# Another order for the middle of a hybrid mixer: spectrum, inverse, second transform and query products

## What is computed

```python
for l in range(2):
    x = x + 0.5 * swiglu_ffn(rms_norm(x, ffn1_norm), w_gate, w_up, w_down)
    proj = rms_norm(x, mix_norm) @ w_in
    y_hy = hyena_mixer(proj[hy_in], ...)
    y_mla = mla_mixer(proj[cq], proj[ckv], proj[kr], ...)
    y_gla = gla_mixer(proj[q, k, v, gates, r], ...)
    x = x + concatenate([y_hy, y_mla, y_gla]) @ w_out
    x = x + 0.5 * swiglu_ffn(rms_norm(x, ffn2_norm), ...)
return rms_norm(x, final_norm)

def hyena_mixer(...):                  # two long convolutions, by Fourier transform
    v, x1, x2 = split(short_conv(u))
    z = x1 * fft_long_conv(v, kern[:, 0], skip[0])
    y = x2 * fft_long_conv(z, kern[:, 1], skip[1])
    return rms_norm(y, out_norm)

def mla_mixer(...):                    # 4 heads; q, k = 128 plain + 64 rotated columns
    q = rms_norm(cq) @ w_uq;  q_rope = rope(q[..., 128:])
    k, v = rms_norm(ckv) @ w_ukv;  k_rope = rope(kr)
    return rms_norm(softmax(q @ k.T * scale) @ v, out_norm)

def gla_mixer(...):                    # gated linear attention, forward and backward
    ...                                # decays: running sums of gate logarithms
```

## Time and profile before

| | before |
|---|---|
| median of 3 runs | 1040.7 us (1040.04 to 1040.89) |
| the profiled execution | 1040.12 us, of which 1038.1 us are its span |
| TensorE busy | 1010.4 us (97%) |
| VectorE, ScalarE, GpSimd busy | 637.3, 485.4, 111.6 us |
| granted TensorE clock | full in all 40 slices |
| the middle of layer 1, 258 to 332 us: TensorE busy | 68.92 of 74 us |
| the middle of layer 2, 768 to 842 us: TensorE busy | 68.92 of 74 us |

### The profile page before, as it was taken

The page is one execution under the profiler, slowest core; times in us unless marked ns, Lnnn a source line. Parts: engine busy times, 40 slices in busy tenths (PEclk is TensorE's granted clock), DMA queues, the critical chain, the costliest instruction groups (busy, mean ns, idle before and its releaser), DMA issues.

```text
span 1038.1 us, 17426 instructions
## 1 busy us (share of the span) xinstructions
PE 1010.4 (97%) x7004; PEld 923.8 (89%) x7004; DVE 637.3 (61%) x738; ACT 485.4 (47%) x663; POOL 111.6 (11%) x160
## 2 busy tenths in 40 slices
PE   7999999999899999999999999999998999999997
PEld 6999999888778999999999999997886889999996
DVE  4655555676886655555566555557679765555555
ACT  6544434356654544343354443434566554434342
POOL 2000000150331100000020000003315220000001
PEclk9999999999999999999999999999999999999999
DMA  9565455444303554555555545552542245455551
GB/s 306 188 227 203 167 197 181 143 163 150 135 22 142 202 202 168 197 179 184 183 178 203 203 167 197 179 185 86 199 164 80 81 148 218 167 197 178 186 182 41
DMA packets 27084, 175.93 MB, mean 169 GB/s; under 512 B 3200, under 2 KB 3712, under 8 KB 6560
## 3 DMA queue, kind: packets, MB, share of 16 engines
q1 hardware_dynamic: 25744, 172.90, 46.5%
q0 software_dynamic: 720, 1.95, 0.7%
q10 hardware_dynamic: 576, 0.45, 0.2%
HBM read 174.58 MB, written 1.05 MB: 169 GB/s over the span
## 4 chain that ended last, share of the span: by engine, by line
issue 50%; PE 38%; POOL 9%; DVE 1%; DMA 1%; POOLq 1%; ACT 0%; SPq 0%; DVEq 0%; ACTq 0%
PE psum L1036 13%; PE psum L1037 13%; PE psum L1038 13%; POOL mixer_scratch L350 3%; POOL mixer_scratch L371 1%; POOL mixer_scratch L370 1%; DMA x<-in_x_dram 1%; POOL statistics L323 1%; POOL statistics L321 1%; POOL statistics L334 0%; POOL x_normed L375 0%; DVE x L727 0%; POOL statistics L337 0%; POOLq L226 0%; POOL mixer_scratch L372 0%
## 5 line engine op out<-in xcount | busy, mean ns | idle before, releaser
L681 DVE TENSOR_TENSOR w_low<-w_raw,w_high 128x2048 fp32r<-128x2048 f32 (+1 forms) x160 | 362.8, 2271 | 198.5 <-ACT w_high L409 198.5
L1036 PE MATMUL psum<-xT_high,w_high 128*128 128x256 f32 x1536 | 437.8, 285 | 1.7 <-DVE xT_low L691 1.6
L1037 PE MATMUL psum<-xT_low,w_high 128*128 128x256 f32 x1536 | 435.3, 283 | 0.0
L1038 PE MATMUL psum<-xT_high,w_low 128*128 128x256 f32 x1536 | 435.2, 283 | 0.0
L409 ACT ACTIVATE w_high<-w_raw 128x2048 fp32r<-128x2048 f32 (+1 forms) x160 | 299.1, 1874 | 99.1 <-PE psum L1038 96.3
L1036 PEld LDWEIGHTS psum<-xT_high,w_high 128*128 128x128 f32 x1536 | 295.2, 192 | 5.8 <-issue 4.0
L1037 PEld LDWEIGHTS psum<-xT_low,w_high 128*128 128x128 f32 x1536 | 295.4, 192 | 1.9 <-issue 0.5
L1038 PEld LDWEIGHTS psum<-xT_high,w_low 128*128 128x128 f32 x1536 | 295.4, 192 | 0.0
L457 ACT ACTIVATE silu_gate<-hidden 128x256 f32<-128x256 f32 x88 | 36.8, 418 | 298.9 <-DVE hidden L706 298.9
L1036 PE MATMUL psum<-w_high,hT_high 128*128 128x512 f32 (+1 forms) x360 | 140.0, 389 | 0.0
L1037 PE MATMUL psum<-w_low,hT_high 128*128 128x512 f32 (+1 forms) x360 | 139.7, 388 | 0.0
(11 more groups left out here) (180 smaller groups left out, 801.9 us busy)
## 6 DMA issues: line engine op xcount, KB each, us to landing
w_raw<-in_w_dram SPq DMA_DIRECT2D x160, 1024.0 KB, 4.8
w_raw<-in_w_dram SPq DMA_DIRECT2D x8, 256.0 KB, 7.9
x<-in_x_dram SPq DMA_DIRECT2D x2, 512.0 KB, 5.8
mixer_scratch<-in_fil_dram POOLq DMA_DIRECT2D x2, 512.0 KB, 6.6
out_dram<-x_normed SPq DMA_DIRECT2D x3, 256.0 KB, 2.1
mixer_scratch<-in_fil_dram POOLq DMA_DIRECT2D x2, 352.0 KB, 6.3
mixer_scratch<-in_fin_dram SPq DMA_DIRECT2D x1, 512.0 KB, 5.5
dft<-in_dft_dram SPq DMA_DIRECT2D x1, 256.0 KB, 5.1
```

The source lines that it names most:

```text
L681: e.tensor_tensor(filled(WL[p], n), filled(raw[p], n), filled(WH[p], n).bitcast(F32), ALU.subtract).then_inc(s_lo.sem, 1)
L1036: e.matmul(out, ah, bh, start=start, stop=False)
L1037: e.matmul(out, ah, bl, start=False, stop=False)
L1038: return e.matmul(out, al, bh, start=False, stop=stop)
```

## The change

All functions stay; calls change places, in each of the two layers.

- TensorE: the first `hy_inverse` goes from behind the values to behind the plain queries, ahead of the rope projection. The second `hy_dft` goes ahead of the rope turn (with one more wait, for the rope products, which read the bank that it writes). Heads 2 and 3 of the second query block go ahead of the second `hy_inverse`; heads 0 and 1 stay behind it.
- VectorE: `combine` and `fold` of the first round go ahead of the splits of S_UQR and S_UKV and of `level_qk(0)`; `gated(0)` goes ahead of the rope products. The scaling of the Hyena rows leaves VectorE.
- ScalarE: the copies of the queries go ahead of the first keys' copy and `level_exp(1)`; the second `spectrum_odd` goes ahead of the copy of QR; the second keys' copy goes ahead of the weight copy of S_WO + 1; the scaling of the Hyena rows is taken on, behind `probs_turned(0)`.

```diff
--- before.py
+++ after.py
@@ -615,21 +615,21 @@
                 natural(l, 3, 1, 4)
                 hi(l, S_WO)
                 values_out(1)
+                e.wait_ge(s_used.sem, used(l, S_UQN))
+                for n in range(2):
+                    copy(QN[:, 2 * n:2 * n + 2, :].rearrange("p a b -> p (a b)"), PS[:, 2 + n, :], a_qn)
                 e.wait_ge(a_km.sem, a_km.at(l))
                 copy(KN[:, 0:2, :].rearrange("p a b -> p (a b)"), PS[:, 4, :], a_kn)
                 level_exp(l, 1)
-                e.wait_ge(s_used.sem, used(l, S_UQN))
-                for n in range(2):
-                    copy(QN[:, 2 * n:2 * n + 2, :].rearrange("p a b -> p (a b)"), PS[:, 2 + n, :], a_qn)
                 e.wait_ge(a_vm.sem, a_vm.at(l))
                 copy(VM[:, 0, :], PS[:, 5, :], a_v)
                 copy(VM[:, 1, :], PS[:, 6, :], a_v)
+                spectrum_odd(l, 1, 7)
                 e.wait_ge(a_qtr.sem, a_qtr.at(l))
                 copy(QR.rearrange("p a b -> p (a b)"), PS[:, 2, :], a_qre)
-                spectrum_odd(l, 1, 7)
-                hi(l, S_WO + 1)
                 e.wait_ge(s_used.sem, used(l, S_UKV))
                 copy(KN[:, 2:4, :].rearrange("p a b -> p (a b)"), PS[:, 1, :], a_kn)
+                hi(l, S_WO + 1)
                 level_exp(l, 2)
                 e.wait_ge(g_ls.sem, g_ls.at(l, 1))
                 copy(AD.rearrange("p h t c -> p h (t c)"), PS[:, 0:4, 0:256], g_la)
@@ -642,6 +642,11 @@
                 probs(l, 0)
                 level_exp(l, 5)
                 probs_turned(l, 0)
+                e.wait_ge(h_r.sem, h_r.at(l))
+                for t in range(T):
+                    v = xn[:, t, 0:256]
+                    r = e.activation(v, v, ACT.Copy, scale=st[:, T_RH + t:T_RH + t + 1])
+                r.then_inc(h_yy.sem, 1)
                 level_exp(l, 6)
                 probs(l, 1)
                 turned_high(l, 2, 0, Y_BANKS[0], Y_TILES[0], C_GO, by_parity)
@@ -946,11 +951,12 @@
                 lo(l, S_UQN)
                 join(l, 0, 0)
                 multiply(l, 0)
-                lo(l, S_UQR)
-                level_qk(l, 0)
-                lo(l, S_UKV)
                 combine(l)
                 fold(l)
+                lo(l, S_UQR)
+                lo(l, S_UKV)
+                level_qk(l, 0)
+                gated(l, 0, 0)
 
                 e.wait_ge(s_used.sem, used(l, S_UQR))
                 q = PS[:, 7, :].rearrange("p (t h d) -> p t h d", t=T, h=H)
@@ -963,7 +969,6 @@
                 e.tensor_tensor(t1, q, rp(0, 0, 64), ALU.mult)
                 e.tensor_tensor(t2[:, :, :, 0:32], q[:, :, :, 32:64], rp(1, 0, 32), ALU.mult)
                 e.tensor_tensor(t2[:, :, :, 32:64], q[:, :, :, 0:32], rp(1, 32, 64), ALU.mult).then_inc(a_qt.sem, 1)
-                gated(l, 0, 0)
                 lo(l, S_WO)
                 level_qk(l, 1)
                 join(l, 1, 6)
@@ -977,11 +982,6 @@
                 score_max(l, 0)
                 level_keep(l, 1)
                 level_qk(l, 4)
-                e.wait_ge(h_r.sem, h_r.at(l))
-                for t in range(T):
-                    v = xn[:, t, 0:256]
-                    r = e.tensor_scalar(v, v, st[:, T_RH + t:T_RH + t + 1], None, ALU.mult)
-                r.then_inc(h_yy.sem, 1)
                 level_keep(l, 2)
                 level_qk(l, 5)
                 score_max(l, 1)
@@ -1303,6 +1303,7 @@
                         r = passes(PS[:, 2 + h // 2, (h % 2) * SEQ:(h % 2 + 1) * SEQ], WH[p][:, k, h * P:(h + 1) * P], WL[p][:, k, h * P:(h + 1) * P],
                                    HH[:, k, :], HL[:, k, :], k == 0, k == 1)
                 r.then_inc(s_used.sem, 1)
+                hy_inverse(l, 0, 0).then_inc(h_inv.sem, 1)
                 e.wait_ge(s_lo.sem, s_lo.at(l, S_UQR + 1))
                 p = pos(S_UQR)
                 for t in range(T):
@@ -1324,18 +1325,18 @@
                     e.wait_ge(g_vr.sem, g_vr.at(l, t + 1))
                     r = passes(PS[:, 5 + t, :], KVH[:, t * P:(t + 1) * P], KVL[:, t * P:(t + 1) * P], WH[p][:, 1, :], WL[p][:, 1, :], True, True)
                 r.then_inc(a_vm.sem, 1)
-                hy_inverse(l, 0, 0).then_inc(h_inv.sem, 1)
                 e.wait_ge(h_oc.sem, h_oc.at(l, 1))
                 keys((2, 3)).then_inc(s_used.sem, 1)
+                e.wait_ge(a_qt.sem, a_qt.at(l))
+                e.wait_ge(a_v.sem, a_v.at(l, 2))
+                e.wait_ge(h_z.sem, h_z.at(l, 1))
+                hy_dft(l, 1, 6)
                 e.wait_ge(a_qr.sem, a_qr.at(l))
                 e.wait_ge(a_qn.sem, a_qn.at(l, 2))
                 for pair in range(2):
                     for t in range(T):
                         r = e.transpose(PS[:, 2, pair * SEQ + t * P:pair * SEQ + (t + 1) * P], xn[:, t, 768 + pair * P:768 + (pair + 1) * P], ident)
                 r.then_inc(a_qtr.sem, 1)
-                e.wait_ge(a_v.sem, a_v.at(l, 2))
-                e.wait_ge(h_z.sem, h_z.at(l, 1))
-                hy_dft(l, 1, 6)
                 e.wait_ge(s_kz.sem, 1)
                 e.wait_ge(a_qre.sem, a_qre.at(l))
                 scores(l, 0, (0, 1))
@@ -1344,13 +1345,15 @@
                 scores(l, 0, (2,))
                 level_scores(l, 0)
                 scores(l, 0, (3,)).then_inc(a_s.sem, 1)
+                e.wait_ge(h_oc.sem, h_oc.at(l, 2))
+                scores(l, 1, (2, 3))
                 hy_inverse(l, 1, 6).then_inc(h_inv.sem, 1)
                 level_scores(l, 1)
                 e.wait_ge(h_z.sem, h_z.at(l, 2))
-                scores(l, 1, (0, 1, 2))
+                scores(l, 1, (0,))
                 level_scores(l, 2)
                 turn_probs(l, 0)
-                scores(l, 1, (3,)).then_inc(a_s.sem, 1)
+                scores(l, 1, (1,)).then_inc(a_s.sem, 1)
                 level_scores(l, 3)
                 attend(l, 0)
                 e.wait_ge(h_yy.sem, h_yy.at(l))
```

## The result

The changed kernel takes **1046.44 us** (median of 5 executions, 1045.76 to 1046.74), the kernel before on the same chip 1040.57 us (5 executions, 1040.04 to 1040.89). The ratio is 1.0057, with a 95% interval of 1.0042 to 1.0071: slower, and the interval leaves out 1. The forecast of 1044.0 had the direction, but the time lies above its range, which ended at 1045.6.

The account below looks back on a forecast made before the run. TensorE, fed without gaps outside the mixer's middle, loses 7.9 us per execution to waits inside it. A loss of 1.8 us a layer, 3.6 in all, gave 1043.7 from the profile or 1044.3 from the median; forecast 1044.0, range 1040.4 to 1045.6.

Parts of the forecast that it names:

- Part 1: First inverse ahead of the rope projection on TensorE: starts at 267.39 without a wait, work behind it 1.72 us late.
- Part 2: GpSimd's level 1 additions and rope sum: held by VectorE's split, so the sum comes at 277.8, bounds 276.1 and 278.4.
- first rival: No hold of the rope sum by the split: sum at 276.1, 0 to 0.4 us a layer, no change; 16%.
- Part 3: Second transform ahead of the rope turn: TensorE waits about 2.0 us for the sum, first scores 2.3 us late at 279.2.
- Part 4: Two query heads ahead of the second inverse: 1.73 us added, inverse 1.9 us late at 286.4, fold wait gone.
- Part 5: Chain behind the second inverse, gated to keep: ends 1.9 us late at 292.5, TensorE waits 2.3 us, then same work.
- Part 6: Hyena scaling from VectorE to ScalarE: frees 0.93 us of VectorE, ends a wait of some 0.2 us ahead of level 3.
- The sum: Whole kernel: 1.9 us late less 0.1 to 0.2 is 1.8 us a layer, 3.6 us in all.
- third rival: More is lost: ScalarE's weight copy delays the first level scores' copy by 0.5; 2.4 to 3 us a layer; 10%.

Follow-up runs that it names:

- e3: Changed kernel with both TensorE waits, ahead of the rope turn and for the keep, filled with repeated work: 1044.05 us.
- e5: Changed kernel with only the wait ahead of the rope turn filled, by four more transform matmuls: 1046.07 us.
- e6: Changed kernel with only the wait for the keep filled, by head 1's product made two more times: 1044.96 us.
- e8: Kernel before with rope sum ahead of level 1, first combine and fold ahead of the slot splits, Hyena scaling on ScalarE: 1040.31 us.
- e10: Kernel before with one move, GpSimd's rope sum ahead of level 1: 1039.78 us.
- e1: Changed kernel with heads 2 and 3 of the second query block back behind the second inverse: 1043.06 us.
- e2: Changed kernel with GpSimd's rope sum ahead of level 1 instead of behind it: 1041.14 us.
- e4: Kernel before with one move, heads 2 and 3 of the second query block ahead of the second inverse: 1041.76 us.
- e7: Changed kernel with heads 2 and 3 back behind the second inverse and the rope sum ahead of level 1: 1038.68 us.
- e11: e2 with the wait for the keep filled, by head 1's product made two more times: 1039.37 us.
- e12: e7 with the scaling of the Hyena rows back on VectorE: 1038.83 us.
- e13: e8 with one head (3) of the second query block ahead of the second inverse: 1038.30 us.

## Why the prediction was wrong in size

By the prediction's own steps, with the trace of after:

- **Part 1** holds: the first inverse starts at 267.38 without a wait. All starts behind it came as reckoned; the values' copies released the transform at 274.03 (reckoned 274.1).
- **Part 2** holds: the split starts at 272.01 (272.1), GpSimd's first addition 0.8 us later. It takes 1.84 us (about 1.9) and ends 0.4 behind the split, and the four together take 3.72 against 2.07 alone; the sum ends at 277.77 (277.8). The first rival (no hold) is excluded. The exclusive lock of the Trainium skill's page "SBUF — State Buffer" ("SBUF: two separate sides") agrees with these 1.84 and 3.72 us.
- **Part 3** holds: turn at 277.82 (277.85), scores at 279.25 (279.2), a wait of 1.83 (about 2.0).
- **Part 4** holds: the second inverse at 286.46 (286.4), and the wait on the fold is gone.
- **Part 5** holds in its starts: gated 288.39, level scores 292.42 (292.5) behind a wait of 2.16 (2.3). It fails in its last sentence: "From there on TensorE has the same work as before". The same work took longer: from 294.0 on, 3.41 us of it ran at half the clock (in layer 2 the 3.41 us began at 792.3, in the scores of Part 3).
- **Part 6** holds in size: from the level scores to the eight turns TensorE took 17.10 us before (290.65 to 307.75); at full clock it now takes 16.93 (after, layer 2) and 16.91 (e3), 0.2 less, as reckoned.
- **The sum** is the step that failed. Its term for the order, 1.8 a layer, measured 1.6 (e3, at full clock): 3.2 us instead of 3.6. The inverse is 1.98 late, but the level scores behind it only 1.78, since the chain between them took 5.96 us instead of 6.17, and Part 6 gives back 0.2 of that. The sum had no term for the clock, and that measured 2.9 us (1.2 and 1.7). 3.2 + 2.9 are the 6.1 us. The third rival had a total near the result (2.4 to 3 a layer), but by another mechanism: the ScalarE delay that it named isn't there. The copy of the first level scores starts 0.79 us behind them, as before, and the second inverse and the level scores behind it came when the sum said.

The reason to look was in the forecast itself. It named two new waits of 2.0 and 2.3 us, where the longest of the middle before is 1.6, and took each at its own length. I had read the clock only as a mean and by 40 slices, and both are too coarse for a fall of 3.41 us.

What is not settled: which executions the clock falls in. e5, e6, e8 and e10 each gave executions with and without a fall, and within one execution the two layers, which repeat one pattern, often differ (e1, e2, e4, e10). The kernel before, with waits of up to 1.6 in the middle, and e3, e7, e11, e12 and e13 have a mean of 0.998 to 0.999 in every execution; no kernel with waits of 1.8 to 2.3 us has. From where on a wait endangers the clock these runs don't say.

## What to carry to other kernels

In this kernel, where several in-order engines hand one chain around, moving TensorE's work ahead of the second inverse, on which the others hang, moved the wait behind it, whole (e4). Read the waits' lengths, not only their sum: two waits of 1.2 and 1.4 us were cheaper than one of 2 us with a short one, and splitting a wait (e13) or even filling it with useless work (e3, e11) gained 1.8 to 2.4 us here. Put the one operation that TensorE waits for ahead of the row of small ones on the same engine, above all where a long operation of another engine holds that engine up: that alone was worth 2 us a layer in the changed order (e2).

## What the runs showed of the hardware that I had not expected

TensorE's clock fell to half behind waits of only 1.8 to 2.3 us, for 3.41 or 6.83 us by its record, mostly while TensorE was busy again; it began between 0.5 us ahead of the wait's end (e5, at 804.8) and 1.6 us after it (after, layer 1). A fall of 3.41 us cost 0.9 us (e10, layer 2 against layer 1), 1.05 (e4), 1.2 and 1.7 (after), one of 6.83 us 2.5 (e1). In e1, e2, e4, e5, e6, e8 and e10 the mean clock differs from execution to execution, and their ranges are 1.7 to 3.9 us, where the kernel before has under 1.4 over 31 executions. Why it fell in one execution or layer and not in another no run here shows.
